# Convolution stage: no modulation pair in the first tile, chunk 3 moved up behind the tap of tile 0, three pairs behind the last tap

## What is computed

```python
mod_lat = (sc @ ada_w[i] + ada_b[i])[:, None, :]      # i = 0, 1: 1024 x 6144 weights each
mod_ctx = scc @ ada_w[i] + ada_b[i]
...
def conformer_conv(h, w_pw1, b_pw1, w_dw, b_dw, ln_g, ln_b, w_pw2, b_pw2):
    u = h @ w_pw1 + b_pw1
    a, g = jnp.split(u, 2, axis=-1)
    v = a * jax.nn.sigmoid(g)
    v = dwconv(v, w_dw, b_dw)                          # 31 taps along the tokens
    v = jax.nn.silu(layernorm(v, ln_g, ln_b))
    return v @ w_pw2 + b_pw2
```

## Time and profile before

| what | us |
|---|---|
| median of 3 runs | 2465.3 |
| lowest and highest run | 2465.12 and 2469.09 |
| profiled execution, its own time | 2467.01 |
| its span, first to last instruction | 2465.2 |
| of it: 8 tiles of the convolution on DVE, first tap to last sum | 76.3 to 269.3 |
| mean of the layer norm on PE | 259.9 to 272.3 |

### The profile page before, as it was taken

The page is one execution under the profiler, slowest core; times in us unless marked ns, Lnnn a source line. Parts: engine busy times, 40 slices in busy tenths (PEclk is TensorE's granted clock), DMA queues, the critical chain, the costliest instruction groups (busy, mean ns, idle before and its releaser), DMA issues.

```text
span 2465.2 us, 36840 instructions
## 1 busy us (share of the span) xinstructions
PE 2269.7 (92%) x14285; PEld 1862.9 (76%) x14285; DVE 1182.5 (48%) x2015; ACT 992.9 (40%) x1650; POOL 817.6 (33%) x395
## 2 busy tenths in 40 slices
PE   4999698999999997989979999989988879999998
PEld 3887477888888885867758888867756767778777
DVE  4699725332043335478554223457565536441541
ACT  5665534332133314378444324444453213431341
POOL 1799231223232221300134444433302103444443
PEclk8999798999999998999989999999998879999999
DMA  8787021222122221200123333333200002333232
GB/s 268 251 271 249 20 69 35 68 63 71 55 60 65 67 65 57 69 10 1 43 78 101 101 88 100 105 92 86 73 1 2 2 1 77 90 102 90 85 102 86
DMA packets 337087, 204.55 MB, mean 83 GB/s; under 512 B 5869, under 2 KB 335159, under 8 KB 336951
## 3 DMA queue, kind: packets, MB, share of 16 engines
q1 hardware_dynamic: 331915, 194.02, 26.0%
q10 hardware_dynamic: 5036, 8.66, 1.1%
HBM read 200.47 MB, written 2.19 MB: 82 GB/s over the span
## 4 chain that ended last, share of the span: by engine, by line
PE 51%; issue 27%; DVE 10%; POOL 8%; ACT 2%; DVEq 1%; SPq 1%; DMA 1%; ACTq 0%; POOLq 0%
PE ps L595 14%; PE ps L596 14%; PE ps L597 14%; POOL w_lo L537 7%; DVE ps L1300 5%; PE ps L1656 1%; PE ps L2673 1%; DVE m L2854 1%; PE ps L1684 1%; PE ps L2660 1%; DMA ada_x<-in_ada_w 1%; PE ps L1392 0%; SPq L698 0%; PE ps L820 0%; PE ps L2669 0%
## 5 line engine op out<-in xcount | busy, mean ns | idle before, releaser
L537 POOL TENSOR_TENSOR w_lo<-raw,w_hi 128x1024 fp32r<-128x1024 f32 (+1 forms) x253 | 646.0, 2554 | 1393.1 <-ACT w_hi L567 1377.2
L595 PE MATMUL ps<-x_hi,w_hi 128*128 128x512 f32 (+1 forms) x1864 | 682.9, 366 | 53.0 <-DVE x_lo L1203 43.7
L596 PE MATMUL ps<-x_lo,w_hi 128*128 128x512 f32 (+1 forms) x1864 | 670.2, 360 | 0.0
L597 PE MATMUL ps<-x_hi,w_lo 128*128 128x512 f32 (+1 forms) x1864 | 669.0, 359 | 0.0
L567 ACT ACTIVATE w_hi<-raw 128x1024 fp32r<-128x1024 f32 (+1 forms) x251 | 280.5, 1118 | 556.2 <-PE ps L597 550.7
L595 PEld LDWEIGHTS ps<-x_hi,w_hi 128*128 128x128 f32 x1864 | 357.9, 192 | 123.2 <-issue 52.3
L596 PEld LDWEIGHTS ps<-x_lo,w_hi 128*128 128x128 f32 x1864 | 358.5, 192 | 53.3 <-issue 3.8
L597 PEld LDWEIGHTS ps<-x_hi,w_lo 128*128 128x128 f32 x1864 | 357.8, 192 | 51.7
L1557 DVE SCALAR_TENSOR_TENSOR f_a<-ps,prm,f_a 128x511 f32<-128x511 f32 (+2 forms) x176 | 116.1, 680 | 356.4 <-ACT f_b L1522 345.5
L595 PE MATMUL ps<-g_hi,w_hi 128*128 128x512 f32 (+1 forms) x704 | 256.9, 365 | 2.1 <-POOL w_lo L537 1.4
L596 PE MATMUL ps<-g_lo,w_hi 128*128 128x512 f32 (+1 forms) x704 | 255.9, 363 | 0.0
(11 more groups left out here) (367 smaller groups left out, 2918.9 us busy)
## 6 DMA issues: line engine op xcount, KB each, us to landing
raw<-in_ffn_w_up SPq DMA_DIRECT2D x88, 512.0 KB, 3.8
ada_tail<-in_ada_w SPq DMA_DIRECT2D x22, 1024.0 KB, 7.5
raw<-in_ffn_w_down SPq DMA_DIRECT2D x32, 704.0 KB, 4.6
raw<-in_w_up SPq DMA_DIRECT2D x44, 512.0 KB, 3.8
ada_s<-in_ada_w SPq DMA_DIRECT2D x20, 1024.0 KB, 7.4
raw<-in_conv_w_pw SPq DMA_DIRECT2D x24, 512.0 KB, 5.9
raw<-in_w_down SPq DMA_DIRECT2D x16, 704.0 KB, 4.6
raw<-in_w_in SPq DMA_DIRECT2D x17, 512.0 KB, 4.0
```

The costliest lines, as they stand in the source:

```text
L537: pool.tensor_tensor(M.w_lo[:, slot, 0:K * P], M.raw[:, slot, 0:K * P], M.w_hi[:, slot, 0:K * P].bitcast(F32), ALU.subtract).then_inc(lo_r ...
L595: pe.matmul(o, wh, hi[:, k, t0:t0 + tn], start=(k == 0), stop=False)
L596: pe.matmul(o, wh, lo[:, k, t0:t0 + tn], start=False, stop=False)
L597: return pe.matmul(o, wl, hi[:, k, t0:t0 + tn], start=False, stop=(k == K - 1))
```

## The change

`PAIRS` becomes (0, 2, 3, 2, 3, 2, 3, 2). The first tile takes no pair, all other tiles keep the count that they had, and pairs 17, 18 and 19 (`BEHIND`) are multiplied behind everything else of the stage. PE makes chunk 2 directly behind the first two chunks, then tap 0 of tile 0, then chunk 3. SP loads block 4 before pair 1, and blocks 5 and 6 without pairs between them. ACT writes no group in tile 0; each later tile writes the group that its own pairs complete, three pairs later than before, and the last two groups stand behind `weights(17)`.

```diff
     REST = 40
-    PAIRS = (3, 2, 3, 2, 3, 2, 3, 2)
+    PAIRS = (0, 2, 3, 2, 3, 2, 3, 2)
+    BEHIND = range(sum(PAIRS), REST // 2)
...
         pair(0)
         w(3)
+        w(4)
         sp.wait_ge(x_ready, done(8))
         pair(1)
-        w(4)
-        pair(2)
         w(5)
-        pair(3)
-        pair(4)
         w(6)
...
             for n in third:
                 pair(n + 2)
+        for n in BEHIND:
+            pair(n + 2)
...
-        first, second, third = pairs_of(0)
         first_two(pe, "pw1", BOTH, "n10")
-        ada(first)
+        chunk(2)
         taps_pe(pe, 0)
-        ada(second)
-        chunk(2)
-        ada(third)
         for j in range(1, 8):
             first, *others = pairs_of(j)
             chunk(2 * j + 1)
...
             for n in others:
                 ada(n)
+        for n in BEHIND:
+            ada(n)
         turn_mods_pe(pe)
...
-            groups_to(pairs_of(j)[1])
+            if j:
+                groups_to(pairs_of(j)[1])
...
         weights(16)
         weights(17)
-        groups_to(pairs_of(7)[-1])
+        groups_to(BEHIND[-1])
         mods_back_act(act)
         copy_conv(act, 7)
```

## The result

| what | us |
|---|---|
| before, median of 6 runs beside it | 2466.54 |
| with the change, median of 6 runs | 2476.09 |
| the same without its one slow run, median of 5 | 2475.70 |
| ratio, 95% interval | 1.004, 1.0029 to 1.0051 |
| profiled execution with the change, own time and span | 2474.89 and 2473.1 |

One of the six runs with the change fell in a slow state (2634.95 us) and is left out of the cost and the ratio. The change costs 2475.70 - 2466.54 = 9.16 us. The prediction had the sign, but 2470.7 was too small: its "+5.4" is little more than half of what was measured, and the range ended at 2473.7.

A forecast was written before the change was run, and what follows sets the result against it. DVE was taken to set the stage's pace and the read-back its end, so DVE's 2.5 us gain counted nothing. The late pairs' chain added 5.4 us to the median 2465.3, giving 2470.7 us, range 2466.8 to 2473.7.

The forecast's parts named there:

- +5.4: End of the stage: the mean, and everything chained behind it, ends 5.4 us later than before.
- The first tile: Convolution's start: 9.4 us of DVE stalls removed, 7.0 paid back by a later first tap, so DVE gains 2.5 us.
- Steps 1 to 3: Stage end: three late pairs and two `pw2` blocks stream unbroken; pair 19 lands at 253.8, the second block at 256.5.
- Step 4: ACT at stage end: `weights(17)` waits for the block until 256.5, groups follow, the last write is issued at 260.5.
- Step 5: Stage end: the write lands in 2.0 us, the read goes out at 262.5, PE starts 2.52 us later, at 265.0.
- Step 6: Mean on PE: starts 0.3 us later, takes 12.42 us as before, ends at 277.7 against 272.34, 5.4 us later.
- Case D: Stage end: a slower stream, or a longer 1.2 GHz stretch in the mean, costs 8.2 us, giving 2473.5; chance 0.16.
- the sum: Stage end: the main forecast, all steps as one chain, 5.4 us later, 2470.7 us; chance 0.60.
- B: Stage end: the blocks do not hold ACT, groups start 1.7 us sooner, loss 3.7 us, 2469.0; chance 0.19.
- C: Stage end: DVE's chain decides instead of the read-back, the mean ends 2.5 us sooner, 2462.8; chance 0.05.

The follow-up runs named there:

- e6: The change with tap 0 of tile 0 ahead of chunk 2 on PE; 2474.20 us against 2466.59 before, ratio 1.003.
- e1: The change with the last two groups ahead of the two weight splits on ACT; 2471.69 us against 2466.37 before, ratio 1.0024.
- e5: The change with 20 thrown away matmuls on PE between pair 19 and the transpose; 2481.35 us against 2466.59 before, ratio 1.0065.
- e9: The change with ten thrown away matmuls on PE between pair 19 and the transpose; 2472.53 us against 2465.95 before, ratio 1.003.
- e4: The change with SP holding the third `pw2` block until the read-back has landed; 2472.19 us, ratio 1.0026 to the kernel before.
- e2: The change with the two `pw2` blocks issued ahead of pair 17 in SP's queue; 2477.34 us against 2466.37 before, ratio 1.0045.
- e8: The change with the transpose of the modulations behind the mean and the groups ahead of the splits; 2464.09 us against 2466.59 before, ratio 0.9994.
- e3: The change without the loads of pairs 17, 18 and 19, PE multiplying old ring contents; 2469.12 us, ratio 1.0014 to the kernel before.
- e12: e10 with six thrown away matmuls on PE ahead of the mean's last step; 2462.91 us against 2466.01 before, ratio 0.9986.
- e10: e8 with tap 0 first and the mean's steps woven between the late pairs; 2462.02 us against 2465.95 before, ratio 0.9986.
- e11: The kernel before with the transpose behind the mean, which also waits for tile 6's copy; 2469.25 us against 2465.95 before, ratio 1.001.
- e7: The change with the three late pairs spread over tiles 1, 3 and 5, groups where they stood before; 2466.51 us against 2466.59, ratio 1.0002.

## Why the prediction was right, and where it was wrong

**The first tile: right, but for one wait.** "7.0 us later than before" for the first tap, at 83.3: it is at 80.78 + 2.27 = 83.05. "DVE gains 2.5 us": 2.84. "No stall at `gated(1)`" and none at tile 1: so it is. e6 shows that the price was the chunk ahead of the tap, and that "2.5 us gained by DVE are worth nothing" holds even for 4.0. What it had at nothing is that PE, further ahead of DVE, now waits 2.5 us ahead of chunk 5 and can be cold behind that: in e1, e5 and e9 DVE got back only 1.7 to 1.9 us. In the change's own trace nothing of the kind happened.

**Steps 1 to 3, the stream: right, 1 us short.** Pair 17 was to land at 242.0, pair 19 at 253.8; PE starts them at (aligned) 242.4 and 254.2. The second block was to be there at 256.5; its split starts at 255.18 + 2.27 = 257.45. I had "PE multiplies it in 1.9 us". Each took 3.05 to 3.64, at 1.2 GHz (0.50 from 242 to 246, where the wait for the transfers leaves PE idle in between). That cost little here: pair 18 was already under way, and the transfers fell only to 293 GB/s from 244 to 246, behind pair 17's end and the issue of pair 19. Over the whole stream, 234 to 254.1, they ran at 356 GB/s and not 384, which fits the 1 us. The Trainium skill tells of this in "TensorE: Matmul & The Clock Gate", HAM oscillation: waits for DMA between short pieces of matmul work let the engine fall back to half clock each time. The trace agrees, with 2.19 to 3.83 us of waiting and 3.05 to 3.64 us for a pair that takes 1.95 elsewhere.

**Step 4, the order on ACT: right.** The groups stand behind the second split, and their last write is issued at 259.08 + 2.27 = 261.35 against 260.5, which is the block's 1 us. That "`weights(17)` has to wait for the block" is what holds them is shown by e1, where the group waits for PE's last pair and no longer for a block.

**Step 5, the read-back: the step that failed first.** I took 2.0 us for a write to land, and then "Before, PE started 2.52 us behind it". Measured are 2.25 and 4.16. The price was copied from a place where nothing else travelled. I had followed SP's queue to the second block and no further, while the splits that step 4 has ahead of the groups free the slots for the third and fourth, just as the writes and the read go out. e4 holds them back and gets 1.34 and 2.24. So the step gave 1.64 us too little for the read and 0.25 for the write. The Trainium skill has the direction in "DMA: Bandwidth & Descriptors", Latency and other measured facts, where access to HBM is slower under high load and so is a DMA's fixed cost; the trace agrees in direction, 3.3 us against 1.7 for the same 40 KB. Whether the time goes in the memory or in the DMA engines that both transfers share, no run here shows.

**Step 6, "takes 12.42 us as before": the step that failed second.** I argued that the mean started cold before and would start cold now, and took the same length. What counts is how long the low clock lasts, not whether it starts there. At 2.4 GHz all through it takes 10.53 us (e9); each us at half clock adds half a us. So before it was cold for 2 x (12.42 - 10.53) = 3.8 us, and with the change for 5.7, and the rows could tell me only of the one. It adds 0.97 in this trace. And nothing in the working had the sums of squares in it, which lost another 1.67 by the clock falling again. How often an execution pays these two is open: e6, nearly as long idle, paid neither, and before, idle for 18 us, had 12.42 and 10.64. Case D's "longer stretch at 1.2 GHz in the mean" was this mechanism, but it was priced as another way to the same 8.2, never beside the sum.

**The terms together.** The transpose came 2.8 us later than predicted (aligned 267.76 against 265.0): 0.85 from the last write, which is the block, 0.25 from its landing and 1.65 from the read's. Then 1.0 for the mean and 1.7 for the sums, less 0.3 in the short steps behind them, makes 5.1, and 5.4 + 5.1 is the +10.4 of the trace to 0.1 us. The medians have 9.16. The block's part was within what the range allowed. The read's landing and the sums had no range of their own at all, and the mean's clock only as a case that excluded the others. In this trace all of them went one way.

**The rivals.** B's 1.7 us met e1's 1.67 by luck (0.8 from the group, 0.9 from the writes), and as a time B was too small: e1 ended 3.8 us below the change, because what is behind it improves too. In the change itself the blocks did land behind pair 19, as the sum had it: PE used the pair at 251.93, ACT the blocks at 253.63 and 255.18. B's way there was not the one I named either: with the blocks landing early (e2) nothing is won, as pair 19 is then late. C is excluded as it stood, but its mechanism is real, and e8 shows it: with the read-back out of the way most of DVE's gain does count, 2.5 us below before by the medians (interval up to 1.0003).

**What stays open.** When the clock falls at the sums of squares. With the change and in e2, e3, e4 and e12 it had been at 1.00 and went to 0.50 within 0.7 us of their start; in e10 and e11 it had not yet come back from the last wait. It did not fall in before, e1, e5, e6, e7, e8 and e9, though the same 2 us of waiting stand ahead of the sums in all of them, and e12 shows that 6 us of work at full clock shortly ahead don't prevent it. The medians differ from the relative numbers of single traces by up to 1.9 us (e10: -3.9 against -2.0; e11 1.5 the other way), which fits falls, here and at chunk 5, that come in some executions and not in others; a second trace of the same kernel would be needed to show that.

## What to carry to other kernels

Work moved behind the last big piece of a stage is paid in full, and what follows it is paid again: the transfers that it now lets run beside it, and, in some executions, the clock of an engine that stood idle. Follow a moved step to the buffers it frees and the loads these release, and give the first work behind an idle gap a range and not its old length: here the mean took 11.96 to 13.43 us behind gaps of 4.9 to 18.2 us, not in the order of the gaps. And before a chain is shortened, take from its end what nothing needs yet: moving the transpose and its wait behind the mean did more than any order of loads.

## What the runs showed of the hardware

- A read of 40 KB of modulations lands in 1.7 us with little or nothing beside it (e1, e3, e4) and in 2.1 to 3.3 beside blocks of 512 KB (e2, e5, e6, e9, the change). The read could be issued 1.35 us behind the last 2 KB write when alone, and 2.2 to 3.1 us beside them.
- At a granted clock of 1.00 throughout, the mean's 6144 columns of float32 take 10.53 us (e9), which is 0.88 us for 512. The thrown away matmuls of 512 took 0.91 each (20 in 18.22 us, ten in 9.07), their first 0.6 to 1.8 us at 0.50.
- Everything from `gated(0)` on stands some 2.3 us sooner or later from one execution to another. In thirteen of the fourteen traces that goes with the granted clock from 34 to 37: 1.00 with the early start, 0.54 to 0.87 with the late one. e5 had 0.50 and the early start, so that pair alone does not decide it.
- The granted clock fell to 0.50 within 0.7 us of the start of the sums of squares (96 matmuls of 128 columns to 6 rows) in five of the fourteen traces (281.9 to 285.1 with the change), while PE's records show it busy throughout; in seven with the same wait ahead of them it did not.
- Behind PE's 2.5 us wait ahead of chunk 5 the granted clock from 104 to 110 was 1.00 in the change's trace and 0.72 in e1, e5 and e9.
